# w_out's middle chunks as one block with three pairs by seven products, and a third pair in each middle block of the down projection

## The reference, cut to what matters

```python
x = x + (u * gate) @ w_out                              # end of layer 0's mixer, w_out 2048 x 2048
x = x + (silu(h @ w_gate) * (h @ w_up)) @ w_down        # both layers, w_down 5632 x 2048
```

## Time and profile before

| | before |
|---|---|
| median of 3 runs | 2071.73 us (2071.61 to 2071.83) |
| profiled execution | 2071.54 us |
| its span, first to last instruction | 2069.8 us |
| TensorE busy | 2062.3 us (100%) |
| VectorE busy | 1694.4 us (82%) |
| ScalarE busy | 1215.4 us (59%) |
| GpSimd busy | 93.4 us (5%) |
| mean DMA rate | 210 GB/s |

### The profile page before, as it was taken

How to read it: one execution, slowest core, us unless ns; L and a number is a source line. 1 busy time by engine, 2 the same in 40 slices (tenths; PEclk the granted TensorE clock), 3 DMA queues, 4 the chain that set the end, 5 groups by cost and what they waited for, 6 DMA issues and landing times.

```text
span 2069.8 us, 24515 instructions
## 1 busy us (share of the span) xinstructions
PE 2062.3 (100%) x9382; PEld 1712.2 (83%) x9382; DVE 1694.4 (82%) x1867; ACT 1215.4 (59%) x1464; POOL 93.4 (5%) x107
## 2 busy tenths in 40 slices
PE   9999999999999999999999999999999999999999
PEld 8888888888888888888888888878888888888887
DVE  5466579999999999988566666579999999999987
ACT  6444556665666656656666665466664666556653
POOL 1000001000000000000011001001000000000000
PEclk9999999999999999999999999999999999999999
DMA  8655547875787757765554455447875787757764
GB/s 326 206 181 171 177 161 217 277 227 186 212 270 228 225 198 235 243 211 202 196 184 168 146 189 174 163 143 227 278 217 195 207 274 219 233 200 233 238 217 149
DMA packets 212384, 434.66 MB, mean 210 GB/s; under 512 B 9169, under 2 KB 9777, under 8 KB 212017
## 3 DMA queue, kind: packets, MB, share of 16 engines
q1 hardware_dynamic: 202848, 398.50, 57.1%
q0 software_dynamic: 9424, 34.65, 8.1%
HBM read 399.56 MB, written 2.10 MB: 194 GB/s over the span
## 4 chain that ended last, share of the span: by engine, by line
PE 97%; DVE 1%; ACT 1%; DMA 0%; issue 0%; SPq 0%; DVEq 0%; ACTq 0%
PE acc L1627 18%; PE acc L1629 18%; PE acc L1628 18%; PE acc L1486 10%; PE acc L1490 10%; PE acc L1488 10%; PE tr L1628 2%; PE tr L1629 2%; PE tr L1627 2%; PE tr L1534 2%; DMA raw<-in_a_w_in_dram 0%; PE tr L1808 0%; PE tr L1597 0%; PE tr L1782 0%; PE tr L1792 0%; DVE a_lo L999 0%
## 5 line engine op out<-in xcount | busy, mean ns | idle before, releaser
L745 ACT ACTIVATE w_hi<-raw 128x1024 fp32r<-128x1024 f32 x312 | 318.0, 1051 | 135.7 <-PE acc L1629 112.9
L1172 DVE TENSOR_TENSOR w_lo<-raw,w_hi 128x1024 fp32r<-128x1024 f32 x252 | 297.9, 1218 | 8.6 <-ACT w_hi L745 8.3
L734 ACT ACTIVATE s_hi<-sums_b 128x1024 fp32r<-128x1024 f32 x216 | 220.7, 1054 | 131.1 <-DVE sums_b L1167 124.3
L1627 PE MATMUL acc<-w_hi,a_hi 128*128 128x512 f32 x736 | 288.1, 391 | 1.3 <-DVE w_lo L1172 1.3
L1629 PE MATMUL acc<-w_hi,a_lo 128*128 128x512 f32 x736 | 286.6, 389 | 0.0
L1628 PE MATMUL acc<-w_lo,a_hi 128*128 128x512 f32 x736 | 286.4, 389 | 0.0
L1486 PE MATMUL acc<-w_hi,a_hi 128*128 128x512 f32 x640 | 254.6, 398 | 0.5 <-DVE a_lo L999 0.5
L973 DVE TENSOR_TENSOR w_lo<-raw,w_hi 128x1024 fp32r<-128x1024 f32 x127 | 154.6, 1234 | 117.0 <-ACT w_hi L583 116.9
L1490 PE MATMUL acc<-w_hi,a_lo 128*128 128x512 f32 x640 | 249.6, 390 | 0.0
L1488 PE MATMUL acc<-w_lo,a_hi 128*128 128x512 f32 x640 | 249.2, 389 | 0.0
L734 ACT ACTIVATE s_hi<-raw 128x1536 fp32r<-128x1536 f32 x108 | 160.5, 1486 | 143.7 <-PE acc L1629 143.7
(11 more groups left out here) (227 smaller groups left out, 3964.2 us busy)
## 6 DMA issues: line engine op xcount, KB each, us to landing
raw<-in_ffn_w_down_dram SPq DMA_DIRECT2D x60, 1024.0 KB, 5.1
raw<-in_ffn_w_gate_dram SPq DMA_DIRECT2D x46, 1024.0 KB, 5.4
raw<-in_ffn_w_up_dram SPq DMA_DIRECT2D x46, 1024.0 KB, 7.0
raw<-in_ffn_w_gate_dram SPq DMA_DIRECT2D x84, 512.0 KB, 4.0
raw<-in_ffn_w_up_dram SPq DMA_DIRECT2D x84, 512.0 KB, 5.5
raw<-in_a_w_in_dram SPq DMA_DIRECT2D x30, 1024.0 KB, 5.1
w_lo<-raw POOLq DMA_DIRECT2D x60, 512.0 KB, 8.1
raw<-in_ffn_w_down_dram SPq DMA_DIRECT2D x56, 512.0 KB, 5.2
```

What stands on the lines that cost most here:

```text
L734: nc.scalar.activation(s_hi[:, operands, :], src, ACT.Copy).then_inc(s_cast, 1)
L745: ins = nc.scalar.activation(w_hi[:, m % RING, :, :], src, ACT.Copy)
L1172: nc.vector.tensor_tensor(w_lo[:, m % RING, :, :], raw[:, slot, half * HG:(half + 1) * HG, :], w_hi[:, m % RING, :, :].bitcast(F32), ALU.s ...
L1627: nc.tensor.matmul(bank[:, :], hi, rhs_hi, start=start, stop=False)
```

## The change

Chunks 1 and 2 of w_out are made as one block, `W_OUT`, with the lists of "down 1" (kind "down wout"), three pairs among them, between the first and the last chunk, which stay plain and now use bank 2. The loop that numbers a block moves into `number_block`, so that w_out has its own list of slots. The middle block of the third part of w_down gets a third pair and new lists. The wait behind both kinds of block is now for two reads, `p1_ready` (ScalarE's read of the first bank) and the new `p6_read` (VectorE's first sum), in place of `gate_ready`.

```diff
-              "down middle": items("g2 g3 g4 g5 s0 u2 u3 s1 u4 u5")}
+              "down middle": items("g3 g4 g5 s0 u3 s1 u4 s2 u5"),
+              "down wout": items("g3 g4 g5 g6 s0 g7 u7 s1 u3 u4 s2 u5 u6")}
...
-             "down middle": loads_of("g2 g3,g4 g5,s0,u2 u3,s1,u4 u5")}
+             "down middle": loads_of("g3 u3,g4 u4,g5 u5,s0,s1,s2"),
+             "down wout": loads_of("g3 g4,g5 g6,s0,g7 u7,s1,u3 u4,s2,u5 u6")}
...
-            with sp.Fori(0, NC) as i:
-                load_unit(w_out_k, i * CH, i * 8 + hg_before["wout"])
...
+            load_unit(w_out_k, 0, hg_before["wout"])
+            n_wout = block_loads(W_OUT, *(w_out_k[:, :, c * CH:(c + 1) * CH] for c in (1, 2)), RAW)
+            for k in range(0, KB, 4):
+                slot_free("wout", n_wout)
...
+            unit(hg_before["wout"], {7: [lambda: gate(NC - 1), lambda: forms_begin(g_hi, g_lo, WINO_H, 0),
+                                         lambda: forms_next(WINO_H),
+                                         lambda: lhs_lo_part(batches["gated"] + NC - 1, g_hi, g_lo, HPC * (NC - 1)),
+                                         lambda: forms_end(WINO_H)]})
+            block_lo(W_OUT, {("g", 3): [lambda: add_residual(hg_before["wout"] + KB // HG, 0, batches["x1"], 0, bank=2)],
+                             ("g", 4): [lambda: forms_lo_part(FORMS[W_OUT], fh_hi[:, :, :], fh_lo[:, :, :], g4_hi, g4_lo)],
+                             ("g", 6): [lambda: dve.wait_ge(forms_lo, FORMS[W_OUT]), lambda: block_sums(W_OUT, 0, before_wout)],
+                             ("s", 0): [lambda: x1_lo(0)], ("u", 7): [lambda: block_sums(W_OUT, 1, before_wout)],
+                             ("u", 4): [lambda: block_sums(W_OUT, 2, before_wout)]})
...
-                    middle = {("g", 2): [lambda: forms_lo_part(FORMS[km], fh_hi[:, 0:len(pairs(km)), :], fh_lo[:, 0:len(pairs(km)), :],
-                                                                        in_place(h_hi, h_spare(p)), in_place(h_lo, h_spare(p)))],
-                              ("g", 4): [lambda: dve.wait_ge(forms_lo, FORMS[km]), lambda: sums(km, 0)],
-                              ("u", 3): [lambda: sums(km, 1)]}
+                    middle = {("g", 3): [lambda: forms_lo_part(FORMS[km], fh_hi[:, :, :], fh_lo[:, :, :], in_place(h_hi, h_spare(p)),
+                                                               in_place(h_lo, h_spare(p)), h4_hi[:, :, :], h4_lo[:, :, :])],
+                              ("g", 5): [lambda: dve.wait_ge(forms_lo, FORMS[km]), lambda: sums(km, 0)],
+                              ("u", 3): [lambda: sums(km, 1)], ("u", 4): [lambda: sums(km, 2)]}
...
-                        middle.update({("g", 3): [lambda: add_residual(end, 0, b_end, NC, bank=2, norm=norm)],
+                        middle.update({("g", 4): [lambda: add_residual(end, 0, b_end, NC, bank=2, norm=norm)],
...
+            def banks_read(k):
+
+                pe.wait_ge(p1_ready, NUMBER[k] + 1)
+                pe.wait_ge(p6_read, NUMBER[k] + 1)
...
-                    pe.wait_ge(gate_ready, NUMBER[km] + 1)
+                    banks_read(km)
```

More of the change, by code:

```diff
@@ L128, in yoco_kernel, with number_block, last_unit_reads @@
     hg_before = {"v": 0, "u": NC * KB // HG, "wout": 2 * NC * KB // HG}
-    hg, n_pair, n_both = 3 * NC * KB // HG, 0, [0] * RAW
+    hg, n_pair, n_both = hg_before["wout"] + KB // HG, 0, [0] * RAW
+    W_OUT = "wout", "down", 0, "wout"
+    def number_block(k, reads, hg, n_pair):
+        NUMBER[k] = len(NUMBER)
+        PAIRS_BEFORE[k] = n_pair
+        for item in order(k):
+            if item[0] == "s":
+                PAIR_OF[k, item[1]] = n_pair
+                n_pair += 1
+            else:
+                HG_OF[k, item] = hg
+                if item in ADDED[kind(k)]:
+                    ADDED_HG.append(hg)
+                hg += 1
+        LAST_PAIR[k], END_OF[k] = n_pair - 1, hg
+        for load in loads(k):
+            slot = len(reads) % RAW
+            n_both[slot] += len({m for m, _ in load}) > 1 or load[0][0] == "s"
+            for item in load:
+                LOAD_OF[k, item], BOTH_OF[k, item] = len(reads) - RAW, n_both[slot]
+            reads.append([("pair", PAIR_OF[k, item[1]] + 1) if item[0] == "s" else
+                          ("added", HG_OF[k, item]) if item in ADDED[kind(k)] else
+                          ("half group", HG_OF[k, item] + 1) for item in load])
+        return hg, n_pair
+    def last_unit_reads(hg):
+        return [[("half group", hg - 6 + 2 * n)] for n in range(RAW)]
+    SLOT_READ["wout"] = last_unit_reads(hg)
+    FORMS[W_OUT] = 1
+    hg, n_pair = number_block(W_OUT, SLOT_READ["wout"], hg, n_pair)
+    hg_before["wout last"] = hg
+    hg += KB // HG
     for layer in range(2):
         reads = SLOT_READ[layer]
-        reads += [[("half group", hg - 6 + 2 * n)] for n in range(RAW)]
+        reads += last_unit_reads(hg)
         for p, (c0, c1) in enumerate(PARTS):
@@ L146, in yoco_kernel @@
                     continue
-                NUMBER[k] = len(NUMBER)
                 if k[2] == 0 if k[1] == "chunk" else k[3] != 1:
                     FORMS[k] = len(FORMS) + 1
[L150 to L169, removed]
+                hg, n_pair = number_block(k, reads, hg, n_pair)
+        assert len(reads) % RAW == 0
         if layer == 0:
+            assert hg % RING == 0
             hg_before["qkv"] = hg
@@ L766, in place_fourth, with read_p1, block_hi, x1_hi @@
                 nc.scalar.activation(in_place(a_lo, 4), f4_lo.bitcast(F32), ACT.Copy).then_inc(fourth_placed, 1)
+            def read_p1(k):
+                act.wait_ge(s_used, 3 * (LAST_PAIR[k] + 1))
+                nc.scalar.activation(sums_b[:, 0, :], acc[2][0][:, :], ACT.Copy).then_inc(p1_ready, 1)
+            def block_hi(k, hooks, before):
+                for item in ACT_ORDERS.get(kind(k), order(k)):
+                    slot, count = in_slot(LOAD_OF[k, item])
+                    both = BOTH_OF[k, item]
+                    if item[0] == "s":
+                        pair_hi(PAIR_OF[k, item[1]], slot, both, before + count)
+                    else:
+                        load, = [w for w in loads(k) if item in w]
+                        half = load.index(item)
+                        if half == 0 and load[1][0] != item[0]:
+                            plain_hi(HG_OF[k, item], slot, half, s_landed[slot], both)
+                        else:
+                            plain_hi(HG_OF[k, item], slot, half, raw_landed[slot], before + count)
+                    for work in hooks.get(item, ()):
+                        work()
+            def x1_hi(c):
+                lhs_hi_part(batches["x1"] + c, a_hi, HPC * c, FFN0)
+            def save_x1(c):
+                save_chunk(1, c, batches["x1"] + c)
+            unit(hg_before["wout"], landed(1), {3: [lambda: read_u(NC - 1)],
+                                                7: [lambda: lhs_hi_part(batches["gated"] + NC - 1, g_hi, HPC * (NC - 1))]})
+            advance(1)
+            block_hi(W_OUT, {("g", 3): [lambda: forms_hi_part(FORMS[W_OUT], fh_hi[:, :, :], g4_hi)],
+                             ("g", 6): [lambda: save_x1(0)], ("s", 0): [lambda: x1_hi(0)]}, slot_n[0])
+            wout_hooks = {1: [lambda: read_p1(W_OUT)], 2: [lambda: save_x1(1)], 3: [lambda: x1_hi(1)],
+                          4: [lambda: save_x1(2)], 5: [lambda: x1_hi(2)]}
+            for j in range(KB // HG):
+                slot, count = in_slot(len(loads(W_OUT)) + j // 2)
+                plain_hi(hg_before["wout last"] + j, slot, j % 2, raw_landed[slot], slot_n[0] + count)
+                for work in wout_hooks.get(j, ()):
+                    work()
+            advance(NC - 1)
             def feed_forward(layer, norm, last_save, last_lhs):
@@ L785, in hidden_hi @@
                     lhs_hi_part(b0 + c, h_hi, HPC * (c - c0))
[L787 to L801, removed]
                 for p, (c0, c1) in enumerate(PARTS):
@@ L845, in feed_forward @@
                     plain_columns(0, first)
[L846 removed]
+                    block_hi(km, middle, before)
                     plain_columns(NC - 1, last)
@@ new lines, in second_sums, with block_sums @@
+            def second_sums(k):
+                dve.wait_ge(w_used, END_OF[k])
+                step.wait()
+                step.inc(nc.vector.tensor_tensor(sums_b[:, 1:3, :], acc_pair[1][:, :, :], sums_b[:, 1:3, :], ALU.add))
+            def block_sums(k, q, before, added=None):
+                if added is not None:
+                    dve.wait_ge(part_added, added)
+                slot, count = in_slot(LOAD_OF[k, ("s", q)])
+                pair_sums(PAIR_OF[k, q], slot, BOTH_OF[k, ("s", q)], before + count)
@@ new lines, in block_lo @@
+            def block_lo(k, hooks):
+                for item in order(k):
+                    slot, _ = in_slot(LOAD_OF[k, item])
+                    if item[0] == "s":
+                        pair_lo(PAIR_OF[k, item[1]], slot)
```

(27 more changed lines are left out.)

141 lines of the change are left out of this document (64 added, 77 removed).

## The result

The changed kernel takes 2110.54 us (median of 6 runs, 2109.19 to 2111.37), the kernel before 2071.67 in the same session (6 runs, 2071.49 to 2072.13). The ratio is 1.0187, 95% interval 1.0176 to 1.0198: slower by 38.9 us. The forecast was 2110 in 2102 to 2121, slower with 0.94. The profiled execution is the one of 2111.37 us, with a span of 2109.7.

The account below looks back on a forecast made before the run. TensorE, busy 2062.3 of 2069.8 us, was taken as the bound, so new lateness adds time. Layer 0's 20.6 plus layer 1's 19.5 minus w_out's 1.4 gave 38.7 more: 2110 us (+1.9%), range 2102 to 2121.

Parts of the forecast that it names:

- The slots: Middle blocks: four raw slots used in turn, so s1's load waits for u3, s2's for u4, last column's for u5.
- the link: Middle blocks: from the end of u3's split through load, sums and split to s1's first product, 10.4 us.
- Layer 0's waits: Layer 0's middle block: TensorE waits 0.5, 7.5, 6.2, 5.2, then 2.0 at the transposes; 20.6 us in all.
- The sign that I had named: TensorE's waits in the changed profile would name s_lo twice in each layer, at 6 to 8 us.
- w_out: w_out: 9 products less save 2.04 us, waits cost 0.6, so 1.4 us gained.
- The two waits behind the first chunk: w_out: the residual ahead of g4's split and the forms' low parts ahead of g5, about 0.2 us each.
- The sum: Whole kernel: 20.6 + 19.5 - 1.4 = 38.7 us on the profiled execution's 2071.54, giving 2110.2.
- Hidden loads: Rival, middle blocks: loads are hidden anyway since VectorE runs ahead; 2068.9 us, not slower; 5%.
- Shorter links: Rival, middle blocks: links 0.8 us shorter and the bank sum ready with the first half group; 2103 us; 12%.
- w_out's loss: Rival, w_out: forms hold up VectorE, 2 us instead of 0.6, and one late pair of 2.7; 2114 us; 8%.
- Half clock through the last columns: Rival, last columns: some four of six half groups in each layer at 0.453 us a product; 2132 us; 10%.
- The 2 to 5 us more that I put on the clock: Last columns: by the skill's rule the clock falls in the waits, raising the sum some 2 to 5 us.

Follow-up runs that it names:

- the other order: Kernel before plus w_out's block and wait by banks, middle blocks as before, VectorE splitting g before the forms: 2069.67 us, ratio 0.9992.

## Why the prediction was right, step by step

**The slots (the step that carried it).** Right, with 10.4 us for the link. Measured from the end of u3's split (948.21) to s1's first product (958.33): 10.1; VectorE's sums could start 5.6 after the first issue and not 5.9. For s2 it was 9.95 (961.68 to 971.63).

**Layer 0's waits.** Forecast before s0, s1, s2 and the column 0.5, 7.5, 6.2, 5.2, and 2.0 at the transposes; the trace has 0.4, 6.8, 4.2, 3.3. The later ones are shorter because TensorE came 0.5, 1.4 and 1.1 us later than forecast to s1, s2 and the column, the last two times by its slower clock (below), and because the links were shorter, by which the waits ended 0.2, 0.6 and 0.7 early: the column began 50.1 after the block's start, forecast 50.8. In layer 1 48.7, forecast 49.4, with waits of 1.1, 6.0, 3.2 and 4.7. The sign that I had named, waits for s_lo of 6 to 8 us twice in each layer, came true for s1 alone. Then the transposes come 4.71 behind the column's start instead of 2.73, 2.0 as forecast, and layer 1's column takes 1.6 more to the span's end, forecast 1.4. But neither is a wait in the trace, as I had it: both times TensorE fills the time with products at the half clock (below). In all 19.9 and 19.1 us for 20.6 and 19.5.

**w_out.** Forecast 1.4 gained; 1.45 by the trace. The wait behind the split of g is there (0.24, a product at 217.22 and the next at 217.69), and goes with the other order. The two waits behind the first chunk that I had forecast at 0.2 each are not in the list of waits; but the second products of the block's first two half groups (226.28 and 229.15, the first to read w_lo) come 0.07 and 0.11 later than the spacing of 0.23. Of the 2.04 us 0.35 are not explained by the one wait, and some 0.2 not with these two either.

**The sum.** 19.9 + 19.1 - 1.45 = 37.5, and 2.2 at the kernel's start, of this one execution: 39.7 of the 39.9 between the spans. Without the start it is 37.7, the medians say 38.9; the 1.2 between them are not located. (The start may differ from one execution to the next: the shortest of the six, 2109.19, is 37.5 above before. Only one was profiled.) So it is in part luck that the median is within 0.5 us of the forecast: the stretches of the trace are 1.2 below the 38.7.

**The rivals.** Hidden loads: refuted by the two queues. Shorter links: by 0.3 and 0.45 and not by 0.8, and the bank sum came behind both half groups as forecast. w_out's loss: no. Half clock through the last columns: it fell, and stayed for part of them only, below. The 2 to 5 us more that I put on the clock did not come either: it fell in the waits, and cost at most some tenths. (My "every stretch of the trace before is at 1.00" was read too widely: from 2050 to its end it is 0.98.)

**What I missed** has no share in the 38.9 but would have mattered for the advice: I named no rival in which VectorE is the bound once the loads are in time, though the row has it busy for 29.4 of 32.3 us. I argued that it was off the path because nothing waited for it; that was true of the kernel before alone.

## What to carry to other kernels

With a few slots used in turn, write beside each load which item's split frees its slot, and count the time from there to the first use: landing, preparation, the engines' order. A load list that pairs an early item with a late one, as g3 with u3, makes the next load as late as the late item; on paper both lists read the same bytes in the same number of loads. And before work is moved from the bound to an engine that is 90% busy in that stretch, compare what is added there with the spare time of that stretch.

## What the runs showed of the hardware

TensorE's clock fell behind the waits. Windows of the changed kernel: the wait for s1, the first products behind it, and the last column's first half group:

```profile
951.00:958.00 7.00, 0.53 (x3) 0.10 (x1) 4.00 (x4) 2.85 (x3) 0.00 (x0) 0.74 0.27 101
958.30:961.00 2.70, 2.67 (x6) 2.15 (x7) 2.70 (x3) 1.29 (x2) 0.00 (x0) 0.50 0.00 0
984.20:988.80 4.60, 4.58 (x12) 3.21 (x12) 4.50 (x7) 0.00 (x0) 0.00 (x0) 0.63 1.05 405
```

The granted clock is 0.50 (1.2 GHz) in the 2.7 us behind the 6.8 us wait, 6 products there instead of 12, and back at full in the same pair. Not every wait does it: behind layer 1's 3.16 us before s2 it is 1.00 from 2075.7 to 2080. s1's 21 products took 6.22 us (958.33 to 964.55) and not 4.76. It cost next to nothing: the 1.5 us were taken out of the wait that follows, since s2's load does not depend on TensorE, and the 12 products of the last column's first half group took 4.7 where TensorE had to wait until 988.9 anyway, when VectorE has staged x2's second chunk (987.46 to 988.88). In layer 1's column the first six products take 2.70 us and not 1.36; but VectorE, without a pause from 2085.08 on, has the fourth half group split only at about 2097.7, and TensorE, slowed, needs it at 2098.0, so some 0.4 us at most are the clock's. The run with layer 1 as before shows the same for a whole block: there s1 and s2 of layer 0 took 7.7 us each (clock 0.60 and 0.61), and the block 49.9, against 6.2, 6.4 and 50.1 here. That the clock falls once the array has idled is what the Trainium skill says (TensorE: Matmul & The Clock Gate, Part 1: The HAM clock gate), and the trace agrees: 1.00 all through the middle blocks of before, 0.50 behind the longer waits here. Where another chain bounds the stretch, the slower clock is hidden as well.
